# A two-block transformer kernel on one core: the mixing norm's gain vector goes first, and ScalarE sums the first norm over token tiles

## The reference, cut to what matters

```python
def rms_norm(x, g):
    xf = x.astype(jnp.float32)
    y = xf * lax.rsqrt(jnp.mean(xf * xf, axis=-1, keepdims=True) + EPS)
    return (y * g.astype(jnp.float32)).astype(x.dtype)

h = rms_norm(x, mix_norm_g[l])                  # the first norm
proj = jnp.einsum('bsd,de->bse', h, w_in[l])    # 1024 -> 3080: q, k, v of two attentions, 8 forget gates
fq, fk, fv, flog, dq, dk, dv = jnp.split(proj, offsets, axis=-1)
```

## Time and profile before

| what | us |
|---|---|
| timed executions, three of them | 1409.92, 1410.9, 1411.08 |
| their median | 1410.9 |
| profiled execution, first to last instruction | 1409.4 |
| PE busy in it | 1345.1 |
| PE busy in its first 20 us | 12.62 |
| PE busy from 20 to 40 us | 19.05 |

### The profile page before, as it was taken

The page is one execution under the profiler, slowest core; times in us unless marked ns, Lnnn a source line. Parts: engine busy times, 40 slices in busy tenths (PEclk is TensorE's granted clock), DMA queues, the critical chain, the costliest instruction groups (busy, mean ns, idle before and its releaser), DMA issues.

```text
span 1409.4 us, 19174 instructions
## 1 busy us (share of the span) xinstructions
PE 1345.1 (95%) x6444; PEld 1114.7 (79%) x6444; DVE 691.7 (49%) x1247; ACT 614.8 (44%) x964; POOL 664.7 (47%) x884
## 2 busy tenths in 40 slices
PE   7899999789999999999989879999999999999997
PEld 5877887668888888888779668877778888888887
DVE  6477656672222222121578878666435555552111
ACT  5445555564434342343434544535344444442223
POOL 5432152254655555565455223555655545554551
PEclk9999999999999999999999989999999999999999
DMA  5322231222433332333483212322323333333331
GB/s 160 83 75 68 69 102 49 76 75 75 119 89 104 89 104 82 99 96 98 90 129 102 59 54 68 104 91 86 94 69 116 99 93 100 92 98 96 99 94 60
DMA packets 227535, 127.06 MB, mean 90 GB/s; under 512 B 15972, under 2 KB 223217, under 8 KB 227473
## 3 DMA queue, kind: packets, MB, share of 16 engines
q1 hardware_dynamic: 226960, 126.04, 32.5%
q10 hardware_dynamic: 513, 0.21, 0.1%
HBM read 117.56 MB, written 2.31 MB: 85 GB/s over the span
## 4 chain that ended last, share of the span: by engine, by line
PE 82%; DVE 8%; issue 4%; DMA 3%; ACT 2%; POOL 1%; ACTq 0%; SPq 0%; DVEq 0%; POOLq 0%
PE PS L745 26%; PE PS L747 26%; PE PS L746 26%; DMA RAW<-in_w_in 1%; DVE PTL L1891 1%; POOL WL L717 1%; PE PS L934 1%; PE PS L910 1%; DMA RAW<-in_w_out 1%; DVE PR L1850 1%; PE PS L911 1%; DVE SQ L2047 1%; DVE SS L1615 0%; ACT WH L1168 0%; DVE NM L1856 0%
## 5 line engine op out<-in xcount | busy, mean ns | idle before, releaser
L717 POOL TENSOR_TENSOR WL<-RAW,WH 128x256 fp32r<-128x256 f32 x864 | 659.0, 794 | 713.3 <-ACT WH L1168 713.2
L745 PE MATMUL PS<-XH,WH 128*128 128x512 f32 x1072 | 424.0, 395 | 2.7 <-DVE X L1963 1.8
L1168 ACT ACTIVATE WH<-RAW 128x1024 fp32r<-128x1024 f32 (+1 forms) x220 | 229.0, 1043 | 450.8 <-PE PS L747 378.0
L747 PE MATMUL PS<-XH,WL 128*128 128x512 f32 x1072 | 418.6, 390 | 0.0
L746 PE MATMUL PS<-XL,WH 128*128 128x512 f32 x1072 | 418.3, 390 | 0.0
L745 PEld LDWEIGHTS PS<-XH,WH 128*128 128x128 f32 x1072 | 202.2, 189 | 44.3 <-DVE X L1963 2.6
L747 PEld LDWEIGHTS PS<-XH,WL 128*128 128x128 f32 x1072 | 201.6, 188 | 43.0
L746 PEld LDWEIGHTS PS<-XL,WH 128*128 128x128 f32 x1072 | 202.0, 188 | 39.5 <-issue 0.7
L745 PE MATMUL PS<-HH,WH 128*128 128x512 f32 (+1 forms) x374 | 141.0, 377 | 0.0
L747 PE MATMUL PS<-HH,WL 128*128 128x512 f32 (+1 forms) x374 | 140.8, 377 | 0.0
L746 PE MATMUL PS<-HL,WH 128*128 128x512 f32 (+1 forms) x374 | 140.8, 377 | 0.0
(11 more groups left out here) (326 smaller groups left out, 1861.9 us busy)
## 6 DMA issues: line engine op xcount, KB each, us to landing
RAW<-in_w_up SPq DMA_DIRECT2D x66, 512.0 KB, 3.8
RAW<-in_w_in SPq DMA_DIRECT2D x60, 512.0 KB, 3.9
RAW<-in_w_down SPq DMA_DIRECT2D x32, 512.0 KB, 3.7
RAW<-in_w_gate SPq DMA_DIRECT2D x22, 512.0 KB, 3.8
RAW<-in_w_out SPq DMA_DIRECT2D x16, 512.0 KB, 3.7
RAW<-in_w_down SPq DMA_DIRECT2D x16, 384.0 KB, 3.3
QB<-QA SPq DMA_DIRECT2D x24, 128.0 KB
KA<-KA SPq DMA_DIRECT2D x24, 128.0 KB
```

Of the source, the lines that this page charges most:

```text
L717: ins = pool.tensor_tensor(WL[:, s, cs], RAW[:, s % 2, cs], WH[:, s, cs].bitcast(F32), ALU.subtract)
L745: pe.matmul(out, ah, bh, start=start, stop=False)
L747: return pe.matmul(out, al, bh, start=False, stop=stop)
L1168: act.activation(WH[:, s, 0:width], RAW[:, s % 2, 0:width], ACT.Copy).then_inc(w_hi, 1)
```

## The change

1. `mix_norm_g` becomes the first of the vectors. Its load has a semaphore of its own (`gain_in`). PE transposes its 8 rows alone, ahead of x, and DVE copies 8 columns. The order of vectors splits one more load, so ACT issues 16.
2. ACT squares the four x tiles as they lie, tokens on partitions (SQT, 128 x 1024), with the sum along the row going to RT. It then makes the norm's factor for 4 numbers per partition (logarithm and exponential) and only then begins with XH. The eight squares SQI and the eight additions on DVE are gone.
3. The high parts of units 0 and 1 are made at other places of ACT's stream: unit 0 after the second square, unit 1 after the second XH.
4. PE makes the first products of unit 0 for four chunks before it touches unit 1. In place of `norm_sum` it makes 4 transposes of RT broadcast along the row, which gives the factors on every partition; DVE copies them to R.
5. The transposes of all the other vectors stand behind the forget gates' products, in place of the transposes of R. DVE copies the other 389 columns ahead of its 11 steps, and ACT waits for them ahead of the high part of unit 4.

```diff
         warm(16)
+        pe.wait_ge(gain_in, 16)
+        pe.transpose(PS[:, ACC + 1, 0:8], ROWV[0:8, 0, :], IDF[0:8, 0:8]).then_inc(vec_t, 1)
         for t in range(TC):
...
-            if t == 1:
-                pe.wait_ge(rows_in, 16 * len(vec_loads))
-                for i in range(4):
-                    r = min(P, n_vec - i * P)
-                    ins = pe.transpose(PS[:, ACC + 1, i * P:i * P + r], ROWV[0:r, i, :], IDF[0:r, 0:r])
-                ins.then_inc(vec_t, 1)
...
+        pe.wait_ge(vec_ready, 1)
+        pe.wait_ge(w_hi, 1)
+        first_products(0, [0])
+        for k in (1, 2):
+            pe.wait_ge(acc_free, k)
+            for t in range(TC):
+                ins = x_transpose(5 + k, t)
+            ins.then_inc(part_ready, 1)
+            first_products(0, [k])
+        first_products(0, [3])
+        pe.wait_ge(w_hi, 2)
+        first_products(1, range(4))
+        for k in range(4, KD):
+            for i in range(2):
+                first_products(i, [k])
...
-        norm_sum(8)
+        pe.wait_ge(rstd_tokens, 1)
+        for t in range(TC):
+            ins = pe.transpose(PS[:, SCO, t * P:(t + 1) * P], RT[:, t:t + 1].broadcast_to([P, P]), IDF[:, :])
+        ins.then_inc(norm_ps, 1)
...
-        pe.wait_ge(r_ready, 1)
-        rt_transposes(R)
+        pe.wait_ge(rows_in, 16 * (len(vec_loads) - 1))
+        for i in range(4):
+            r = min(P, n_vec - i * P)
+            ins = pe.transpose(PS[:, OB, i * P:i * P + r], ROWV[0:r, i, :], IDF[0:r, 0:r])
+        ins.then_inc(vec_t, 1)
         v_tile("v1", 0)
...
-        for s in range(2):
-            hi_part(0, s)
+        for t in range(TC):
+            act.wait_ge(x_in[t], 16)
+            act.activation(SQT[:, t, :], XTM[:, t, :], ACT.Square, accum_out=RT[:, t:t + 1]).then_inc(sq_tokens, 1)
+            if t == 1:
+                hi_part(0, 0)
+        act.wait_ge(sq_tokens, TC)
+        act.wait_ge(dve_made, 1)
+        act.activation(RT[:, :], RT[:, :], ACT.Ln, bias=BT[:, 0:1], scale=1.0 / D).then_inc(ln_done, 1)
+        act.wait_ge(ln_done, 1)
+        act.activation(RT[:, :], RT[:, :], ACT.Exp, scale=-0.5).then_inc(rstd_tokens, 1)
         act.wait_ge(vec_ready, 1)
...
-        rstd(R[:, :], 1, 1.0 / D, PS[:, SCO, :])
+        act.wait_ge(vec_ready, 2)
...
+        dve.wait_ge(norm_ps, 1)
+        dve.tensor_copy(R[:, :], PS[:, SCO, :]).then_inc(r_ready, 1)
+        dve.wait_ge(vec_t, 2)
+        dve.tensor_copy(VEC[:, 8:], PS[:, OB, 8:n_vec]).then_inc(vec_ready, 1)
+        dve.wait_ge(vec_ready, 2)
         step(dve.tensor_tensor(GG[:, :], vcol("final_norm_g", 0, 8), vcol("norm1_g_2", 0, 8), ALU.mult))
```

More of the change, by code:

```diff
@@ L296, in program @@
     consts_in = sem("consts_in")
+    gain_in = sem("gain_in")
     rows_in = sem("rows_in")
@@ L317, in program @@
     low_done = sem("low_done")
+    sq_tokens = sem("sq_tokens")
     sq_ready = sem("sq_ready")
@@ L321, in program @@
     ln_done = sem("ln_done")
+    rstd_tokens = sem("rstd_tokens")
     r_ready = sem("r_ready")
@@ L834, in _, with first_products @@
                 warm(6)
-            if t == 1:
-                pe.wait_ge(rows_in, 16 * len(vec_loads))
-                for i in range(4):
-                    r = min(P, n_vec - i * P)
-                    ins = pe.transpose(PS[:, ACC + 1, i * P:i * P + r], ROWV[0:r, i, :], IDF[0:r, 0:r])
-                ins.then_inc(vec_t, 1)
[L843 to L852, removed]
+        def first_products(i, ks):
+            for k in ks:
+                pe.wait_ge(low_done, k + 1)
                 w = WH[:, i, k * P:(k + 1) * P]
@@ L1062, in down @@
                     ins.then_inc(w_used, 1)
-        pairs_with_norm("ffn1", 16, L0["out1"])
+        pairs_with_norm("ffn1", 8, L0["out1"])
         down("down1", L0["ffn1"])
         first_pair(UN["cab"], TL["cab"], XH, XL, low(L0["down1"]))
-        norm_sum(32, 0)
+        norm_sum(24, 0)
         pe.wait_ge(ss_mixed, 1)
-        norm_sum(32, 1)
+        norm_sum(24, 1)
         for i in range(2, 8):
@@ L1117, in token_sums @@
         def token_sums(h):
-            pe.wait_ge(ss_done, 51)
-            pe.wait_ge(sq_ready, 52 + h)
+            pe.wait_ge(ss_done, 43)
+            pe.wait_ge(sq_ready, 44 + h)
             for t in range(2 * h, 2 * h + 2):
@@ L1193, in _ @@
             act.dma_start(ROWV[n % P:n % P + k, n // P, :],
-                          d[name].rearrange("(a b) -> a b", b=P)[r0:r0 + k, :]).then_inc(rows_in, 16)
-        for s in range(2):
-            hi_part(0, s)
+                          d[name].rearrange("(a b) -> a b", b=P)[r0:r0 + k, :]).then_inc(rows_in if n else gain_in, 16)
+        for t in range(TC):
[8 more added lines that the diff above has]
+        act.activation(RT[:, :], RT[:, :], ACT.Exp, scale=-0.5).then_inc(rstd_tokens, 1)
         act.wait_ge(vec_ready, 1)
-        act.wait_ge(dve_made, 1)
         for c in range(KD):
             act.wait_ge(part_ready, c + 1)
-            src = PS[:, init_bank(c), :]
-            act.activation(XH[:, c, :], src, ACT.Copy, scale=vcol("mix_norm_g", c)).then_inc(act_done, 1)
-            act.activation(SQI[:, c, :], src, ACT.Square).then_inc(sq_ready, 1)
+            act.activation(XH[:, c, :], PS[:, init_bank(c), :], ACT.Copy, scale=vcol("mix_norm_g", c)).then_inc(act_done, 1)
+            if c == 1:
+                hi_part(0, 1)
             if c in (5, 7):
@@ L1376, in residual_tiles @@
                 gain_and_square(TL[name] + c, c, vcol(gain, c), sq0, c)
-        residual_tiles("out1", "ffn_norm_g", 8, lambda c: [UN["out1"] + c // 2] if c % 2 else [])
+        residual_tiles("out1", "ffn_norm_g", 0, lambda c: [UN["out1"] + c // 2] if c % 2 else [])
         def swiglu_group(i):
@@ L1484, in _ @@
             act.activation(MH2[:, c, :], tile_t(TL["conv_out"] + c), ACT.Copy).then_inc(act_done, 1)
-        residual_tiles("out2", "norm2_g_2", 36, lambda c: [UN["out2"] + c])
+        residual_tiles("out2", "norm2_g_2", 28, lambda c: [UN["out2"] + c])
         rstd(R[:, :], 5, 1.0 / D, PS[:, SCO, :])
@@ L1634, in _ @@
         dve.wait_ge(vec_t, 1)
-        dve.tensor_copy(VEC[:, :], PS[:, ACC + 1, 0:n_vec]).then_inc(vec_ready, 1)
+        dve.tensor_copy(VEC[:, 0:8], PS[:, ACC + 1, 0:8]).then_inc(vec_ready, 1)
         dve.wait_ge(vec_ready, 1)
@@ L2011, in _ @@
                                   ALU.subtract).then_inc(low_done, 1)
[L2012 to L2017 removed]
+                add_square(8 + 2 * k + 1, k, 0, 0)
+                add_square(8 + 2 * k + 2, k, 1, 1)
+        dve.wait_ge(ss_done, 24)
         dve.scalar_tensor_tensor(out=SS[:, 1, :], in0=SS[:, 0, :], scalar=EPS, in1=SS[:, 1, :], op0=ALU.mult,
@@ L2081, in _ @@
             conv_taps(3, n_early)
-        rt_copy(2)
+        rt_copy(1)
         dve.wait_ge(bv_in, 16)
```

33 lines of the change are left out of this document (14 added, 19 removed).

## The result

| what | before | after |
|---|---|---|
| timed executions (four each) | 1409.76 to 1411.08 | 1418.74 to 1420.1 |
| median, us | 1410.41 | 1418.84 |
| profiled span, us | 1409.4 | 1416.9 |

What follows compares the result with a forecast made beforehand. PE's order of work was taken to bound the kernel. Terms 1.4 - 0.4 + 6.0 + 2.2 = 9.2 us gave span 1418.6 and, with the median 1.5 above it, 1420.1 us; range 1416.8 to 1423.0.

Steps and rivals of the forecast that it cites:

- the large term: Before the first v tile: PE stands while DVE copies vectors, runs its 11 steps and drains the q tile; 6.0 us.
- front, to the low-weight products: From the start to PE's low-weight products: later first XH and some half clock; 1.4 us late, from 0.3 to 2.0.
- norm's sum, and the rest to where PE is ready for the v tiles: After the low-weight products: the norm's two passes (0.86) become four transposes (0.44); 0.4 us saved.
- the new wait: PE's stand before the first v tile: copy 0.57, steps 4.45, drain 0.69, handovers 0.3; 6.0 us, from 5.7 to 6.3.
- the clock behind it: Half clock on PE after its stand before the v tiles; costs 2.2 us, from 1.6 to 2.8.
- given back later: After the v tiles: their later start goes through to the end one for one, nothing swallowed at transfer KB<-CR; 0 us.
- The rival of a costlier table switch: ACT's two table switches ahead of the first XH each take another 1.28 us; time 1422.7; chance 0.05.
- the steps, 36.15 - 31.70 = 4.45: DVE's 11 steps ahead of the q tile's drain, no longer covered by the gates' products; 4.45 us of PE's wait.
- the v tiles aren't held: Rival: DVE gets the vectors early, so PE's v-tile start isn't held and only the front is left; 1408.6; chance 0.03.
- no half clock follows: Rival: behind the wait before the v tiles the clock falls late or returns at once; 1416.8 to 1417.9; chance 0.09.
- the delay is swallowed at the transfer: Rival: KB<-CR ahead of the first scores has its own clock time, absorbing 6.5 of 9.2 us; 1413.6; chance 0.04.
- second wait: Rival: PE also waits at the gates' chain or longer at the first scores; 2 to 4 us more; chance 0.07.

Runs made afterwards that it cites:

- e10_front_warm: Changed kernel with 36 unneeded identity transposes on PE behind the last x tile's blocks, where PE stands; 1418.35 us, ratio to the kernel before 1.0057.
- e1: Changed kernel with DVE's copy of the other vectors and its three readers moved behind the q and k drains and gates' row; 1409.69 us, ratio to before 0.9998.
- e2: Changed kernel with PE's transposes of the other vectors moved ahead of the gates' 24 products, DVE's stream untouched; 1409.81 us, ratio to before 0.9998.
- e5: Changed kernel with the eight of DVE's 11 steps that read no vector moved ahead of the wait for the vectors; 1414.13 us, ratio to before 1.0032.
- e7: Kernel before with only parts 1 and 5 of the change, the old norm and transposes of R kept; 1419.46 us, ratio to before 1.0073.
- e6_both_mended: Changed kernel with DVE's vector copy and its readers behind the drains, and the factor's logarithm and exponential behind the last XH; 1405.29 us, ratio to before 0.9967.
- e4: Changed kernel with ACT's high part of unit 4 held until the q and k tiles are drained, keeping POOL quiet; 1418.1 us, ratio to before 1.0054.
- e3: Changed kernel with 46 unneeded identity transposes on PE between the transposes of the vectors and the first v tile; 1415.83 us, ratio to before 1.0043.
- e8: e6_both_mended with added identity transposes in PE's three short gaps of the front; 1405.17 us, ratio to before 0.9972.

## Why the prediction was right, and where its terms were off

The time lay within the range, and the direction and the mechanism of the large term were as written. That the total came within 1.3 us is in part luck, since a term that was too small (the wait) and one that I had put at nothing (what was given back) offset each other. Term by term, with what the profiles measured:

| term | forecast, us | measured, us |
|---|---|---|
| front, to the low-weight products | 1.4 | 1.32 |
| norm's sum, and the rest to where PE is ready for the v tiles | -0.4 | -0.15 |
| the new wait | 6.0 | 6.80 |
| the clock behind it | 2.2 | 2.08 |
| given back later | 0 | -2.5 |
| sum, between the profiled spans | 9.2 | 7.5 |

*The front.* The first XH came at 16.62, earlier than the 17.1 of the forecast; the pace of a square was 1.05 (8.37 to 9.42), with the read of its sum half hidden, and not my 1.15:

```profile
8.37 1.06 ACT L1216 ACTIVATE SQT<-XTM 128x1024 f32<-128x1024 f32 x1
9.33 0.19 ACT L1216 ACTIVATION_READ_ACCUMULATOR SQT<-XTM 128x1 f32 x1
9.42 1.04 ACT L1216 ACTIVATE SQT<-XTM 128x1024 f32<-128x1024 f32 x1
...
13.60 1.28 ACT L1221 ACT_TABLE_LOAD   x1
14.89 0.30 ACT L1221 ACTIVATE RT<-RT,BT 128x4 f32<-128x4 f32 x1
15.21 1.28 ACT L1223 ACT_TABLE_LOAD   x1
16.50 0.21 ACT L1223 ACTIVATE RT<-RT 128x4 f32<-128x4 f32 x1
```

The table loads cost 1.28 each, with an activation 0.01 behind each; of the drain that the Trainium skill ("ScalarE: Activation LUTs", What ACT_TABLE_LOAD costs) adds to every switch, nothing is to be seen here either. The term of 1.4 came out at 1.32, but its two parts did not: the half clock in the front cost 1.49 by e10_front_warm, where I took 1.1, and without it the front would have been 0.17 early, where I had 0.3 late. The support I gave for the half clock was loosely put, since the earlier trace rows show slice means of 0.66 to 0.94, the edges of the dips, and no row of 0.50; the trace has them, from 12 to 15 us and from 67 to 73. The rival of a costlier table switch falls with the rows above.

*The wait.* The mechanism stands (e1, e2, e5, e7). I took the steps at 4.45 us from a stretch in which POOL was idle. ACT had waited for the same copied vectors, and its high part of unit 4 then released POOL's low part right into them. The term that was mis-sized is "the steps, 36.15 - 31.70 = 4.45": 5.33 here, 4.13 with POOL quiet. So two things are wrong with the 4.45. It lacks 1.20 us of contention, and it holds a time in which DVE stood, which the changed kernel doesn't have (there the gap at this place is 0.04):

```profile
32.62 0.23 DVE L1760 CAST IDB<-IDF 128x128 bf16<-128x128 f32 x1 [0.37 <-DVE GD L1758]
```

*What was given back.* I claimed that the delay goes through one for one, because the transfer KB<-CR "moves with the v tiles and swallows nothing that happens earlier". It did go through to the first scores (10.05 at the drain, 10.32 there), but the reason is weaker than I put it. The transfer also depends on when the weight unit's load is issued beside it, and in the changed kernel that load happened to come 10.18 us later too (63.52 and 73.70). In e1_drain_first it came behind the transfer, and 1.28 us of delay were gone at this very place. That the claim held here was luck.

Then 2.3 us went between the first scores and 730 us. Two pieces are seen. Before, the clock was at half from PE's restart at 67.48 to about 73.1; after, it fell only at 78.2, behind the restart at 77.80, and rose at 81.6:

```profile
78.00:79.00 1.00, 1.00 (x5) 0.91 (x5) 0.37 (x3) 0.98 (x2) 1.00 (x2) 0.59 0.06 16
...
81.00:82.00 1.00, 1.00 (x7) 0.91 (x5) 0.23 (x1) 0.00 (x0) 1.00 (x3) 0.70 0.68 158
82.00:83.00 1.00, 1.00 (x6) 0.82 (x5) 0.93 (x4) 0.56 (x2) 0.63 (x1) 1.00 1.12 339
```

Half of the difference, (5.7 - 3.4) / 2, is 1.1 us; the delay of PE's stream falls by 1.0 there, from 10.32 to 9.29. And a transfer RAW<-in_w_out on the chain took 4.46 us before (at 230.71) and after:

```profile
239.58 3.37 DMA RAW<-in_w_out
```

The delay brought neither about: the same transfer took 3.32 to 3.56 in all ten variants, and each of them won 0.6 to 1.3 us against the kernel before right behind the first scores, those too that were not late (e1_drain_first, e6_both_mended). So it is the kernel before that was slow at both places; with one profiled execution of it, whether always or in this one stays open. The last 0.6 us went between 730 and 860 us. What sets the length of that half clock was not tested. The medians, 8.4 apart, give back less than the profiled executions. And my base was 0.5 too high: over four executions the median before is 1410.41, not 1410.9.

*The rivals.* That the v tiles aren't held and that no half clock follows are refuted by the runs. That the delay is swallowed at the transfer did not happen here, but its mechanism is real for a delay of 1.3 us (e1_drain_first). No second wait came behind the first: the gap before the scores was 3.96 against 3.69.

## What to carry to other kernels

Ask of every wait that is added to an in-order stream what stands behind it there, and whether the next piece of work of the very engine that it waits for is among it: if so, the two engines run one after the other, however short each step is. Moving the drains ahead of that wait gave back the 0.68% (to within 0.16%, and with 1.3 us of it from a shorter transfer), and moving the factor's two activations off the path of the first XH made the same idea 0.33% faster than the kernel before. A saving on engines beside the bound (DVE busy for 3.9 us less, ACT for 0.8) was worth nothing in the changed kernel, whose first products waited for ACT's new work and whose v tiles waited for DVE.

## What the runs showed of the hardware that was not expected

- DVE's casts and its 4 x 512 product took 0.66, 0.84 and 1.03 us beside a POOL subtraction, and 0.23, 0.48 and 0.63 without it (e4, e5). In e6_both_mended DVE's casts got longer (0.80 and 0.66 for IDB and IDR, 0.23 elsewhere) while POOL's pieces kept their 2.83 us, so the two engines don't share the loss evenly.
- The transfer KB<-CR ahead of the first scores took 2.80 to 3.27 us where a load of 512 KB had been issued 0.6 to 0.9 us before it, and landed within 0.2 us of that load; it took 1.72 or 1.73 where it was issued first (e1, e3, e5). An order of two issues by another engine was worth 1.3 us on PE's path.
- A gain of 1.0 to 1.5 us from a kept clock is real where it is made (e10, e8) and is not to be found in the time of the whole kernel. In e10 the clock behind the wait before the v tiles was at half again; later dips fall differently in each profile, so a term of this size can't be read from the medians of executions that scatter by 5 us or more.
